# A two-layer trunk of attention, gated convolution and product-key experts: side work spread over more slots, a shorter front, and query weights of the first layer's third and fourth chunk read once for both halves

## The reference: what is computed

```python
for i in range(2):
    hn = rmsnorm(h, norm_mix[i])
    y = diff_attention(hn, w_qkv, ..., w_o) if i == 0 else short_conv(hn, w_in, conv_w, w_out)
    h = h + y
    h = h + peer_ffn(rmsnorm(h, norm_ffn[i]), w_q[i], keys[i], u[i], v[i])

def peer_ffn(x, w_q, sub_keys, u_tab, v_tab):
    q = (x @ w_q).reshape(T, 8, 2, 128)
    s = einsum('thpd,hpkd->thpk', q, sub_keys)      # 8 heads, 2 halves, 128 keys
    s_top, i_top = top_k(s, 16)                     # then the 16 best of 16 x 16 sums
    idx, gates = ..., softmax(best)                 # 8 heads x 16 experts per token
    act = gelu(dot(u_tab[idx], x)) * gates
    return sum over the 128 of act * v_tab[idx]
```

## Time and profile before

| | us |
|---|---|
| median of three runs | 1513.47 |
| the profiled execution | 1514.77 |
| its span | 1512.9 |
| PE busy | 1342.2 |
| DVE busy | 993.3 |
| ACT busy | 596.3 |
| DMA, all transfers | 617.63 MB |

### The profile page before, as it was taken

The page is one execution under the profiler, slowest core; times in us unless marked ns, Lnnn a source line. Parts: engine busy times, 40 slices in busy tenths (PEclk is TensorE's granted clock), DMA queues, the critical chain, the costliest instruction groups (busy, mean ns, idle before and its releaser), DMA issues.

```text
span 1512.9 us, 12565 instructions
## 1 busy us (share of the span) xinstructions
PE 1342.2 (89%) x3294; PEld 570.8 (38%) x3294; DVE 993.3 (66%) x2412; ACT 596.3 (39%) x1805; POOL 585.5 (39%) x518
## 2 busy tenths in 40 slices
PE   9999899899878789999897898999999889878787
PEld 4444344344333333434332333434433333222222
DVE  4677877885656777546488544667767766765454
ACT  1334464643333434334334433343434344343333
POOL 0033334453323343445344433434444444444442
PEclk9999999999999999999999999999999999999999
DMA  9879999999999999999999999999999999999998
GB/s 390 337 293 421 366 423 418 421 413 421 421 423 423 418 421 418 404 412 421 421 417 401 420 416 423 393 424 406 416 421 422 417 417 422 421 411 422 421 421 334
DMA packets 85175, 617.63 MB, mean 408 GB/s; under 512 B 9456, under 2 KB 9584, under 8 KB 13680
## 3 DMA queue, kind: packets, MB, share of 16 engines
q0 software_dynamic: 74016, 536.90, 86.1%
q1 hardware_dynamic: 9360, 72.62, 11.6%
q10 hardware_dynamic: 1728, 7.31, 1.2%
HBM read 615.75 MB, written 1.05 MB: 408 GB/s over the span
## 4 chain that ended last, share of the span: by engine, by line
DMA 40%; PE 36%; DVE 13%; ACT 7%; issue 4%; POOL 1%; SPq 0%; DVEq 0%; POOLq 0%; ACTq 0%
DMA ring<-in_peer_uv_dram,idx 38%; PE acc L670 24%; PE pp L418 10%; DVE ring L1494 7%; ACT diag L1026 2%; DMA ring<-in_w_qkv_dram 2%; ACT weight L1022 1%; ACT L1020 1%; ACT gelu L1020 1%; POOL ring L794 1%; ACT L882 1%; PE tt L433 1%; DVE top_i L1210 1%; ACT work L843 1%; DVE pick L1252 0%
## 5 line engine op out<-in xcount | busy, mean ns | idle before, releaser
L670 PE MATMUL acc<-ring,diag 128*128 128x512 f32 x2048 | 991.6, 610 | 159.8 <-ACT diag L1026 154.4
L794 POOL DMA_INDIRECT ring<-in_peer_uv_dram,idx x510 | 581.3, 1140 | 910.7 <-PE acc L670 799.6
L1494 DVE CUSTOM_DVE_ANT_0 ring<-ring,xf 128x1024 f32<-128x1024 f32 x512 | 627.2, 1226 | 443.3 <-DMA ring<-in_peer_uv_dram,idx 433.7
L670 PEld LDWEIGHTS acc<-ring,diag 128*128 128x128 f32 x2048 | 370.3, 191 | 717.4 <-ACT diag L1026 367.4
L1020 ACT ACTIVATE gelu<-dots 128x1 f32<-128x1 f32 x512 | 103.7, 202 | 795.0 <-DVE dots L1494 792.3
L1026 ACT ACTIVATE diag<-const,weight 128x128 f32<-128x128 f32 x512 | 205.4, 401 | 16.8
L1022 ACT ACTIVATE weight<-gelu,gates 128x1 f32<-128x1 f32 x512 | 150.8, 294 | 16.6
L418 PE MATMUL pp<-stream,xT 128*128 128x512 f32 x144 | 72.5, 594 | 0.0
L418 PE MATMUL pp<-ring,xT 128*128 128x512 f32 (+1 forms) x112 | 46.5, 544 | 1.6 <-DMA ring<-in_w_qkv_dram 1.2
L1494 DVE DVE_READ_ACCUMULATOR2_ANT dots<- 128x1 f32 x512 | 42.2, 82 | 0.0
L418 PE MATMUL pp<-kept,xT 128*128 128x512 f32 x80 | 40.0, 592 | 0.0
(11 more groups left out here) (164 smaller groups left out, 752.0 us busy)
## 6 DMA issues: line engine op xcount, KB each, us to landing
stream<-in_peer_w_q_dram SPq DMA_DIRECT2D x14, 1024.0 KB
ring<-in_peer_uv_dram,idx POOLq DMA_INDIRECT x510
stream<-in_w_qkv_dram SPq DMA_DIRECT2D x4, 1024.0 KB
ring<-in_w_qkv_dram SPq DMA_DIRECT2D x2, 2048.0 KB, 26.7
stream<-in_w_o_dram SPq DMA_DIRECT2D x4, 1024.0 KB
ring<-in_peer_w_q_dram SPq DMA_DIRECT2D x2, 2048.0 KB, 32.2
kept<-in_peer_w_q_dram SPq DMA_DIRECT2D x2, 2048.0 KB
spare<-in_conv_w_in_dram SPq DMA_DIRECT2D x2, 2048.0 KB, 14.6
```

Source lines behind the costliest of these rows:

```text
L670: mm = nc.tensor.matmul(acc[half][:, :], diag[:, s % RING, :], row[:, D + half * 512:D + (half + 1) * 512], start=(k == 0), stop=(k == SLO ...
L794: nc.gpsimd.indirect_dma_start(dst, None, uv_dram, bass.IndirectOffsetOnAxis(idx[:, at:at + 1], 0)).then_inc(landed, 16)
L1494: nc.vector.tensor_tensor_reduce(row[:, 0:D], row[:, 0:D], xf[:, s // SLOTS % 2, :], 1.0, 0.0, ALU.mult, ALU.add, dots[:, s % RING:s % RIN ...
```

## The change

1. **Front, PE.** Of the 8 steps of the second half's input 0, all of which stood ahead of the first head's scores, 4 now stand ahead and 4 behind; the second head and input 4 follow. The attention of the first half is interleaved at other places with inputs 4 and 5. The last four steps of the first query chunk wait for the columns of `xT` one by one (`f_column_copied`), not for all four.
2. **Front, others.** The second half's `xT1` is scaled by POOL, before its first gather, and no longer by DVE. ACT copies key 1 before value 4, and y before value 5.
3. **Query chunks.** `QUERY_ORDER` lets the second half compute chunks 2, 3, 1, 0 in this order. Chunks 2 and 3 are shared with the first half: 2 stays in the stream place from the first half's use to the second's, 3 in place 7 as before. One 2 MB load goes.
4. **Places.** Since the stream is held by chunk 2, input 3 of window 1 loads to place 7, and output 1 to place 6, which is free only when the second half's values are mixed (slot 78).
5. **Positions.** In window 1's side work input 5 goes ahead of late chunk 2, `RANK_PIECES` for the first window are 1.5 and 1 rather than 2, the norms of the queries and keys have their own slots (`LATE_NORM`); in window 2's side work the inputs stand 10 slots apart, no longer 8; in window 3's the outputs 5 apart, no longer 4.

```diff
-    dict(q0=12, k0=22, q1=30, k1=54,
+    dict(q0=12, k0=28, q1=31, k1=58,
...
-LATE_RANK_PROJECT = {1: 0, 2: 25, 3: 50}
+LATE_RANK_PROJECT = {1: 0, 2: 34, 3: 59}
+QUERY_ORDER = {1: (2, 3, 1, 0)}
-RANK_PIECES = {(0, 1): 2, (0, 2): 2, (0, 3): 1, (1, 0): 2, (2, 2): 1.5}
-LATE_IN_PROJECT = {2: 9, 1: 17, 5: 33, 3: 41}
-SHARED = {(1, "in", 0), (1, "in", 4), (1, "in", 5), (1, "out", 0), (1, "wq", 3),
+RANK_PIECES = {(0, 1): 1.5, (0, 2): 1.5, (1, 0): 2, (2, 0): 1.25, (2, 2): 1.15, (3, 0): 1.25}
+LATE_IN_PROJECT = {2: 9, 1: 17, 5: 26, 3: 43}
+LATE_NORM = {2: 24, 1: 27, 3: 54}
+SHARED = {(1, "in", 0), (1, "in", 4), (1, "in", 5), (1, "out", 0), (1, "wq", 0), (1, "wq", 1),
...
+def chunk_of(n, what, c):
+    return QUERY_ORDER[n][c] if what == "wq" and n in QUERY_ORDER else c
...
-        loads += [(0, "wq", 2, STREAM), (1, "in", 3, STREAM), (0, "wq", 3, 7),
-                  (1, "out", 1, STREAM), (1, "wq", 0, STREAM), (1, "wq", 1, STREAM), (1, "wq", 2, STREAM)]
-        loads += [(2, "in", 2, 6), (2, "out", 0, 8), (2, "in", 4, STREAM), (2, "in", 3, 7), (2, "out", 1, 9), ...
+        loads += [(0, "wq", 2, STREAM), (1, "in", 3, 7), (0, "wq", 3, 7), (1, "out", 1, 6)]
+        loads += [(2, "out", 1, 9), (2, "out", 0, 8), (2, "in", 2, 6), (1, "wq", 2, STREAM), (2, "in", 3, 7), (1, "wq", 3, STREAM),
...
-                project_part(pp, 0, "in", 5, xT, range(3, KT))
-                pe.wait_ge(x_scaled, 3)
-                project_part(ff, 1, "in", 0, xT1, range(0, 2))
                 turn_y(0, 0)
-                project_part(ff, 1, "in", 0, xT1, range(2, 3))
+                pe.wait_ge(x1_scaled, 1)
+                project_part(ff, 1, "in", 0, xT1, range(0, 1))
...
+                for k in high:
+                    if k < KT - 1:
+                        pe.wait_ge(f_column_copied, k)
+                    else:
+                        copied(pe, tt, (0, "f", 1))
+                    project_part(pp, 0, "wq", 0, xT, (k,), slice(0, 256), "a")
...
+            pool.wait_ge(const_in, 16)
+            pool.wait_ge(x_cols_in[1], 16)
+            nc.gpsimd.tensor_tensor(xT1, xT1, gain_mix[:, 0:KT].unsqueeze(2).to_broadcast([P, KT, P]), ALU.mult).then_inc(x1_scaled, 1)
...
-                dve.wait_ge(x_cols_in[1], 16)
-                scale_columns(xT1, 1, 0, KT)
...
-                at = LATE_IN_PROJECT[c] + 9
+                at = LATE_NORM[c]
```

More of the change, by code:

```diff
@@ L357, in held, with reader_after @@
         def held(n, what, c):
-            return held_at[(n - 1 if (n, what, c) in SHARED else n, what, c)]
+            if (n, what, c) in SHARED:
+                return held_at[n - 1, what, chunk_of(n, what, c)]
+            return held_at[n, what, c]
+        def reader_after(n, what, c):
+            return next(((n + 1, what, later) for later in range(6) if (n + 1, what, later) in SHARED and chunk_of(n + 1, what, later) == c), None)
         def weights(n, what, c, k):
@@ L420, in project_part @@
                         mm.then_inc(pool.written_sem(key), 1)
-                    elif k % DEEP == DEEP - 1 and held(n, what, c)[0] == STREAM:
+                    elif k % DEEP == DEEP - 1 and held(n, what, c)[0] == STREAM and reader_after(n, what, c) is None:
                         mm.then_inc(part_used, 1)
@@ L548, in front @@
                 project_part(pp, 0, "out", 1, yT, low)
-                project_part(ff, 1, "in", 0, xT1, range(3, 4))
                 turn_y(0, 1)
-                project_part(ff, 1, "in", 0, xT1, range(4, 5))
+                project_part(ff, 1, "in", 0, xT1, range(1, 2))
                 copied(pe, tt, (0, "y", 1))
@@ L676, in _ @@
             front()
-            sides = begun(late(1), late_input(2), turn_late("q", 0), late_input(1), turn_late("k", 0), attention(0), late(2),
-                          turn_late("q", 1), late_input(5), late_input(3), turn_late("k", 1), late(3), turn_mixed(0), attention(1), turn_mixed(1),
+            sides = begun(late(1), late_input(2), turn_late("q", 0), late_input(1), turn_late("k", 0), attention(0), late_input(5),
+                          turn_late("q", 1), late(2), late_input(3), turn_late("k", 1), late(3), turn_mixed(0), attention(1), turn_mixed(1),
                           output(1), turn_output(1), *(experts(1, c) for c in range(4)))
@@ L692, in matrix_of @@
             def matrix_of(n, what, c):
[L693 removed]
+                return {"in": in_dram[n // 2], "out": out_w_dram[n // 2], "wq": peer_w_q[n // 2]}[what][chunk_of(n, what, c)]
             def last_reader(n, what, c):
[L697 to L698 removed]
+                if reader_after(n, what, c):
+                    return reader_after(n, what, c)
                 return n, "wqb" if (n, what, c) == (0, "wq", 0) else what, c
@@ L820, in copy_scaled @@
                     ins = nc.scalar.activation(dst[:, j, :], tt.bank(key)[:, j * P:(j + 1) * P], ACT.Copy, scale=columns[:, j:j + 1])
+                    if j < 3 and key[0:2] == (0, "f"):
+                        ins.then_inc(f_column_copied, 1)
                 ins.then_inc(tt.read_sem(key), 1)
@@ L1090, in scale_for_mixer, with scale_columns @@
                 dve.sem_inc(mix_scaled, 1)
-            def scale_columns(dst, b, first, last):
+            def scale_columns(dst, first, last):
                 gain = gain_mix[:, first:last].unsqueeze(2).to_broadcast([P, last - first, P])
```

58 lines of the change are left out of this document (29 added, 29 removed).

## The result

The changed kernel takes 1505.27 us, the median of four runs (1504.36 to 1506.13), against 1513.59 before: a ratio of 0.9939 with a 95% interval of 0.9925 to 0.9952, so 8.3 us less by the medians and 9.2 by the ratio. The profiled execution took 1505.94, its span 1504.1, 8.8 less than before. The forecast was 1501.9, with a range of 1495.5 to 1509.5: faster, as forecast, by 8.3 instead of 11.6.

What follows compares the result with a forecast made beforehand. The kernel was taken as bound by DMA bytes at 421 GB/s plus 46 us of gaps, with PE close behind. Terms summed to -11.6 us from 1514.77, so 1503.2, or 1501.9 as median; range 1495.5 to 1509.5.

Steps and rivals of the forecast that it cites:

- one load less: Second half's query chunk 2 no longer loaded: 2.097 MB at 421 GB/s, -5.0 us.
- front: Gap from 60 to 100 us: four steps moved behind the scores, -3.5, less three waits; first gather earlier, -2.6 us.
- slots 27 to 38: 160 to 200 us: spreading DVE's ranking and norm regains part of 5.0 us lost; -3.0, bounds 2.6 lost to 5.0 regained.
- what is new in window 0: Late chunk 2's ranking in slots 54 to 56 and output 1's load from slot 78: +1.0 us, between 0 and 5.
- windows 1 and 2, distances: Inputs 10 slots apart instead of 8 ease PE; a third of 9.6 us regained: -3.0, bounds 0 and -9.6.
- windows 1 and 2, ranking: Chunk 0's ranking at 1.25 steps a slot makes DVE denser in slots 105 to 117: +1.0 us, between 0 and 3.
- the three waits: PE in the front: key 1's norm +0.3, second half's y +0.4, last query steps +0.2 on the 0.37 us.
- POOL's scaling: Front: POOL scales xT1, ready at 35.5 us, needed at 57; taken as nothing, though a port lock might stop DVE.
- a reserve of gathers: Slots 27 to 38: gathers run 2.6 us ahead while PE does not, so the reserve is smaller by as much.
- the late output chunk: Window 1's output 1 loads from slot 78 for slot 83, five slots or 12.5 us: just in time.
- late chunk 2's ranking beside the norm of key 3: Slots 54 to 56: the same cluster as the old one; with output 1's load together +1.0 us.
- Rival 4: Output 1 of window 1 lands late, PE stands 19.7 us at slot 83; +20.3, 1533.8 us; chance 0.05.

Runs made afterwards that it cites:

- c2: The changed kernel with query chunk 2 loaded a second time for the second half (2.1 MB more); 1511.99 us, ratio 0.9983 to the kernel before.
- c4: The kernel before with only the new front (PE and ACT order, second half's x scaled by GpSimd); 1512.73 us, ratio 0.9986 to the kernel before.
- c3: The changed kernel with chunk 1's ranking back at 2 steps a slot and the late norms at slots 18 and 26; 1509.48 us, ratio 0.9968.
- c5: The changed kernel with the side work of windows 2 and 3 at the slots and densities of before; 1505.09 us, ratio 0.9935.
- c8: The changed kernel with the second half's x scaled by VectorE again and nothing on GpSimd; 1505.08 us, ratio 0.9933.
- c10: The changed kernel with the first half's chunk 3 projected in slots 55 to 62, not 59 to 66, and ranked from slot 68; 1504.89 us, ratio 0.9930.
- a2: The changed kernel itself timed again, as reference beside three variants on one chip; 1506.36 us, ratio 0.9941.
- c9: The changed kernel with output chunk 1 in two transfers and chunk 3's ranking from slot 74 at 1.25 steps a slot; 1505.20 us, ratio 0.9939.

## Why the prediction was right, and where not

The account was right in the main: bytes at the rate of the full windows, and gaps. The term for the second layer was not. Term by term:

| term | forecast | measured |
|---|---|---|
| one load less | -5.0 | -5.0 by bytes; c2: 6.7 with 2.5 us of doubt |
| front | -2.6 | -2.6 of gap; gather 2.2 earlier; c4: 2.1 |
| slots 27 to 38 | -3.0 | -5.0 of gap; c3: 4.4 |
| what is new in window 0 | +1.0 | +3.1 of gap |
| windows 1 and 2, distances | -3.0 | -1.0 of gap from 500 to 1100; c5: none |
| windows 1 and 2, ranking | +1.0 | +1.0 of gap from 1100 to 1300; c5: none |
| sum | -11.6 | -9.5 of gap, -8.8 of span, -8.3 of median |

**The load** went as worked out. **The front**: the three waits came at 0.17, 0.41 and 0.46 instead of 0.3, 0.4 and 0.57. The scores are 2.21 us earlier and not 2.6: the waits added 0.67 (0.17, 0.41 and 0.09 over the 0.37 of before), less than the 0.9 that I had added, so by them the gain should have been larger. It came out smaller because a wait costs more than the idle time in its row. A step still takes its 0.86 us (the eight from 91.60 on are followed at 98.57). But when nothing is waited for, PE starts the next operation 0.16 us before the recorded end of the last, and at each wait this overlap is lost; the four transposes behind a wait took 0.66 and not 0.60. The two waits that are new make 0.4 us of it, and most of the 0.6 that the sum lacks. Such waits also made me wrong on the loop: I had its start within 0.5 us of before, and with four waits where one was, PE's first expert comes 1.15 us later and slot 8's gather at 104.67 instead of 103.52. Nothing was lost by it, since the gathers in flight covered it (424 GB/s from 100 to 110). **POOL's scaling** costs 1.89 us at 35.48 and nothing to the time (c8). By the rule of the Trainium skill, "SBUF — State Buffer", section "SBUF: two separate sides", it could have stopped VectorE. In this trace VectorE does nothing between 35.16 and 37.52 us, and GpSimd's operation ends at 37.37, so the two did not meet. In c10 they overlap by 0.36 us, and VectorE's operation takes 0.42 us and GpSimd's 1.89, as they do alone; but that operation has one input in PSUM (`ss`), so the rule's case, two inputs in SBUF, is met in no run here.

**Slots 27 to 38** came out at the far end of my bounds. I had found the cause (two long operations beside a norm) and then took off 2 us for a reserve of gathers that the earlier front would use up. That subtraction was the error, and c4 shows it: DVE was waiting for rows at 118 and 120 us, so the loop was not PE's there, and earlier rows moved it by most of the gain, 1.7 of 2.3 us by slot 27. A step that waits now and then for the very thing that is made earlier follows it; to say that it "starts no earlier" holds for its first slot only.

**What is new in window 0** was the term too small by 2 us. The prediction had the mechanism of the late output chunk, and called it just in time: it landed in 12.4 us as reckoned (11.4 and 14.6 were the rows), but the five slots that I had put at 12.5 us, the pace of the gathers, took PE 8.5: their rows had landed and no steps stood between, so that PE ran five experts on end from 316.87 to 325.6. Hence the wait of 4.0 us. The other cost named, late chunk 2's ranking beside the norm of key 3, came as well, with a wait of PE of 3.49 us at 254.64, and no transfer time was lost around it (421 GB/s from 240 to 290). Of the other mechanism, late chunk 3 with its scores and ranking on top of the second attention's exponentials, it had nothing: I followed the ranking of chunk 2 into slots 54 to 56 and did not follow chunk 3 into 66 to 72. I had looked for two lists of steps that meet on one engine; here ACT, PE and DVE each meet something, and each waits in turn. Rival 4 was this wait with the price of the 32.2 us row, which had stood in a queue at the start; 4.0 us of it cost some 0.6, if that.

**Windows 1 and 2**: I took PE's 2.6 us a slot against 2.5 for the cause of the dips and a third of 9.6 us for the gain. c5 moves all these positions back and the time stays. The two rows of the table cannot be told apart by their windows: the ranking of window 1 lies in 500 to 1100 (755 to 789 us), that of window 2 at 1109 to 1140 us, and what follows to 1300 has neither. Their sum, nothing instead of -2.0, is what was measured. From 900 to 1100 alone the changed kernel lost 3.3 us in one profile and 410 GB/s, 5.2 us, in another (a2), so the term was smaller than the scatter of the rows it was read from.

**Luck** is part of how near the sum came: slots 27 to 38 gave 2.0 us more than forecast, and what is new in window 0 cost 2.1 more, so that these two misses cancel and only the 2.0 of the second layer is left of the three.

## What to carry to other kernels

Where the DMA engines are full, price each stretch as transfer time missing against the full rate; a gap from one cluster of work shows there, and goes when the cluster is spread. Whether a faster start survives is read from the waits behind it: where the loop waits for rows, the gain goes through. When steps are moved out of one crowd, list for every engine what now stands at the place they go to: beside the 5.0 us won at one place stand 3.1 lost at another. And a wait seen in the trace is not yet a price: those of 3.5 and 4.0 us here cost nothing and 0.6 of transfer time, while 2.6 us were lost where PE did not wait at all.

## What the runs showed of the hardware

After a wait PE sometimes runs at half pace. The four matmuls of an expert take 1.98 us behind a short wait, at a granted clock of 1.00, the level of 2.4 GHz. Behind the wait of 2.95 us at 294.57 they took 3.45, with a granted clock of 0.51 from 294.6 to 297.6, so at the level of 1.2 GHz. It is not tied to the length of the wait alone. In a2 the same four took 3.78 us behind a wait of 3.50, in c9 1.98 behind one of 3.49:

```profile
254.68 3.78 PE L686 MATMUL acc<-ring,diag 128*128 128x512 f32 x4 [3.50 <-ACT diag L1047]
```

```profile
255.76 1.98 PE L691 MATMUL acc<-ring,diag 128*128 128x512 f32 x4 [3.49 <-ACT diag L1057]
```

The granted clock is 0.50 there in a2 and 1.00 in c9. So a stall can cost 1.8 us more than its length in the next four matmuls alone, and in a2 the transposes and the expert behind them are slow too (1.06 for 0.60 us and 2.73 for 1.88). Whether it does differs from one execution to the next.

ACT loads a function table in 1.28 us each time that it goes from gelu to exponentials and back, so four exponentials of 128x256 between two experts take 4.7 us of it, 2.6 of them loads.

GpSimd took 1.89 us for a 128x1024 product that VectorE does in 1.22, with the engine free ahead of it.
